# The experts' weighted sum of a two-block transformer kernel, from feature-major to token-major

## The reference, cut to what matters

```python
def peer_ffn(h, peer_wq, peer_subkeys, peer_u, peer_v):
    ...
        expert = jnp.take_along_axis(ids, pos, axis=-1)
        g = jax.nn.softmax(top_s, axis=-1).astype(hb.dtype)
        u_sel = peer_u[expert]
        a = jax.nn.gelu(jnp.einsum('bqhkd,bqd->bqhk', u_sel, hb))
        v_sel = peer_v[expert]
        return jnp.einsum('bqhk,bqhkd->bqd', g * a, v_sel)
...
        x = x + gate2 * peer_ffn(h2, peer_wq, peer_subkeys, peer_u, peer_v)
```

## Time and profile before

| | us |
|---|---|
| median of three runs (lowest, highest) | 1178.29 (1177.71, 1179.69) |
| the profiled execution: own time | 1180.36 |
| its span, first to last instruction | 1178.4 |
| PE busy in the span | 1051.1 (89%) |
| VectorE, ScalarE, GpSimd busy | 837.5, 433.0, 268.8 |
| TensorE's mean granted clock, of full speed | 0.972 |

### The profile page before, as it was taken

The page is one execution under the profiler, slowest core; times in us unless marked ns, Lnnn a source line. Parts: engine busy times, 40 slices in busy tenths (PEclk is TensorE's granted clock), DMA queues, the critical chain, the costliest instruction groups (busy, mean ns, idle before and its releaser), DMA issues.

```text
span 1178.4 us, 18884 instructions
## 1 busy us (share of the span) xinstructions
PE 1051.1 (89%) x7587; PEld 980.2 (83%) x7587; DVE 837.5 (71%) x1801; ACT 433.0 (37%) x913; POOL 268.8 (23%) x289
## 2 busy tenths in 40 slices
PE   8999987999999987777877778878999999999997
PEld 6999986998899877777877777778899888898886
DVE  7978889667667667666776766655756868765776
ACT  3635832123212221222122122211557654476452
POOL 1000005343334333333333333434000000300000
PEclk9999999999999999998999999989999999999999
DMA  9965988999999999999999999999854655455540
GB/s 371 406 244 180 348 313 307 420 421 420 421 420 420 421 420 421 420 421 420 420 420 421 420 421 422 420 422 420 325 208 161 237 205 184 147 211 179 186 171 36
DMA packets 59480, 390.35 MB, mean 331 GB/s; under 512 B 6785, under 2 KB 7809, under 8 KB 15618
## 3 DMA queue, kind: packets, MB, share of 16 engines
q0 software_dynamic: 36864, 268.45, 55.0%
q1 hardware_dynamic: 21056, 120.10, 27.8%
q10 hardware_dynamic: 1474, 0.60, 0.2%
HBM read 388.08 MB, written 1.05 MB: 330 GB/s over the span
## 4 chain that ended last, share of the span: by engine, by line
PE 63%; DMA 24%; DVE 6%; ACT 4%; issue 1%; SPq 0%; another core or an unknown queue 0%; DVEq 0%; ACTq 0%
DMA rows<-in_peer_uv,work 23%; PE aux L1566 23%; PE pj L1609 6%; PE pj L1611 5%; PE pj L1610 5%; PE aux L1545 5%; PE pj L1286 5%; PE pj L1287 4%; PE pj L1288 4%; DVE rows L2061 2%; DMA rows<-in_w_ada 1%; PE aux L1360 1%; ACT work L1142 1%; ACT rows L1010 1%; PE aux L1425 1%
## 5 line engine op out<-in xcount | busy, mean ns | idle before, releaser
L1566 PE MATMUL aux<-work,rows 128*128 128x128 f32 x2080 | 263.4, 291 | 73.8 <-ACT work L1142 73.8
L1566 PEld LDWEIGHTS aux<-work,rows 128*128 128x128 f32 x2080 | 256.2, 206 | 81.6 <-ACT work L1142 81.4
L1566 PE MATMUL aux<-work,low_pairs 128*128 128x128 f32 x2016 | 238.2, 279 | 30.2 <-ACT work L1142 30.1
L1566 PEld LDWEIGHTS aux<-work,low_pairs 128*128 128x128 f32 x2016 | 233.0, 195 | 34.0 <-ACT work L1142 34.0
L898 POOL DMA_INDIRECT rows<-in_peer_uv,work x130 | 125.5, 965 | 301.2 <-PE aux L1566 232.1
L707 DVE TENSOR_TENSOR wlo<-wring,whi 128x1024 fp32r<-128x1024 f32 x100 | 121.0, 1235 | 77.6 <-ACT whi L701 77.1
L898 POOL DMA_INDIRECT low_pairs<-in_peer_uv,work x126 | 118.3, 939 | 158.5 <-PE aux L1566 153.4
L1286 PE MATMUL pj<-xh,whi 128*128 128x256 f32 x512 | 146.3, 286 | 0.4
L1137 ACT ACTIVATE work<-work 128x4 f32<-128x4 f32 (+2 forms) x71 | 14.7, 207 | 358.3 <-DVE work L2061 358.3
L1287 PE MATMUL pj<-xl,whi 128*128 128x256 f32 x512 | 144.8, 283 | 0.0
L1288 PE MATMUL pj<-xh,wlo 128*128 128x256 f32 x512 | 144.8, 283 | 0.0
(11 more groups left out here) (288 smaller groups left out, 1461.5 us busy)
## 6 DMA issues: line engine op xcount, KB each, us to landing
wring<-in_w SPq DMA_DIRECT2D x76, 1024.0 KB, 4.8
rows<-in_w_ada SPq DMA_DIRECT2D x40, 512.0 KB, 10.1
low_pairs<-in_w_ada SPq DMA_DIRECT2D x1, 4096.0 KB, 13.4
rows<-in_w SPq DMA_DIRECT2D x3, 1024.0 KB, 10.4
rows<-in_peer_uv,work POOLq DMA_INDIRECT x130
work<-in_late_rows SPq DMA_DIRECT2D x2, 1024.0 KB, 7.5
xT<-in_gate_rows SPq DMA_DIRECT2D x2, 1024.0 KB, 7.2
rows<-in_norm_rows SPq DMA_DIRECT2D x2, 1024.0 KB, 7.3
```

The costliest lines, as they stand in the source:

```text
L1566: ins = mm(peer_sum[t][:, c * P:(c + 1) * P], pair(n)[:, D + c * P:D + (c + 1) * P], diag[:, n % PICKS, :], start=(n % (EXPERT_HEADS * PIC ...
```

## The change

The diagonal becomes the weights and v the stream: two products of 512 columns for a pair, so the sum has tokens as rows. At a tile's end it is turned back: ScalarE copies the first 512 columns of the sum from PSUM into `hT` (free by then), VectorE the other 512, TensorE turns each half with four transposes into two banks of PSUM, and `join` reads those. For tile 0 the copies come at the end of group 8, the transposes ahead of group 10's sums and the join behind group 10 (before: behind group 9). For tile 1 the first half is turned right behind the last sum, the second between the parts 3 and 4 of vg. ScalarE's copy waits for the first of the last pair's two products alone.

```diff
 def sum_pair(t, n):
     pe.wait_ge(diag_ready, n + 1)
-    for c in range(KC):
-        ins = mm(peer_sum[t][:, c * P:(c + 1) * P], pair(n)[:, D + c * P:D + (c + 1) * P], diag[:, n % PICKS, :],
-                 start=(n % (EXPERT_HEADS * PICKS) == 0 and c % 4 == 0), stop=False, skip_group_check=True)
+    of_tile = n % (EXPERT_HEADS * PICKS)
+    last = of_tile == EXPERT_HEADS * PICKS - 1
+    for c in range(2):
+        ins = mm(peer_sum[t][:, half(c)], diag[:, n % PICKS, :], pair(n)[:, D + c * 512:D + (c + 1) * 512],
+                 start=(of_tile == 0), stop=last, skip_group_check=True)
+        if last and c == 0:
+            ins.then_inc(sum_first_half, 1)
     ins.then_inc(pair_used, 1)
+
+def turn_sum(t, c):
+    pe.wait_ge(sum_out[c], t + 1)
+    for q in range(4):
+        ins = nc.tensor.transpose(aux[:, 2 + c, q * P:(q + 1) * P], hT[:, 4 * c + q, tile_of(t)], ident[:, :])
+    ins.then_inc(sum_turned, 1)
...
+                if g == EXPERT_HEADS + 2:
+                    turn_sum(0, 0)
+                    turn_sum(0, 1)
...
             pe.wait_ge(const_ready, 13)
+            pe.wait_ge(x_ready, KC)
+            turn_sum(1, 0)
...
-                    rows_pass(l, use("vg", 0), *x_tile(l, 0), at_=(2, 3))
+                    rows_pass(l, use("vg", 0), *x_tile(l, 0), at_=(2, ))
+                    turn_sum(1, 1)
+                    rows_pass(l, use("vg", 0), *x_tile(l, 0), at_=(3, ))
...
+def sum_first_half_out(t):
+    act.wait_ge(sum_first_half, t + 1)
+    nc.scalar.copy(quarter(hT, t, 0), by_chunk(peer_sum[t][:, 0:512])).then_inc(sum_out[0], 1)
...
+def sum_second_half_out(t):
+    dve.wait_ge(pair_used, (t + 1) * EXPERT_HEADS * PICKS)
+    v.tensor_copy(quarter(hT, t, 1), by_chunk(peer_sum[t][:, 512:D])).then_inc(sum_out[1], 1)
 def join(t):
     for c in range(KC):
+        if c % 4 == 0:
+            dve.wait_ge(sum_turned, 2 * t + c // 4 + 1)
         x = xT[:, c, t * P:(t + 1) * P]
-        v.scalar_tensor_tensor(x, peer_sum[t][:, c * P:(c + 1) * P], mod[:, 5 * KC + c:5 * KC + c + 1], x, ALU.mult, ALU.add) \
+        v.scalar_tensor_tensor(x, aux[:, 2 + c // 4, c % 4 * P:(c % 4 + 1) * P], mod[:, 5 * KC + c:5 * KC + c + 1], x, ALU.mult, ALU.add) \
             .then_inc(x_ready, 1)
```

More of the change, by code:

```diff
@@ L535, in build @@
         pair_used = sem("pair_used")
+        sum_first_half, sum_out, sum_turned = sem("sum_first_half"), [sem("sum_out_act"), sem("sum_out_dve")], sem("sum_turned")
         x_ready = sem("x_ready")
@@ L1157, in _ @@
                     gate_exps(g + AHEAD)
+                if g == EXPERT_HEADS:
+                    sum_first_half_out(0)
             layer_hi(act, 0, 2, 3)
+            sum_first_half_out(1)
             x0_hi(1)
@@ L2115, in _ @@
                         x0_low(0)
-                if g == EXPERT_HEADS + 1:
-                    dve.wait_ge(pair_used, EXPERT_HEADS * PICKS)
+                if g == EXPERT_HEADS:
+                    sum_second_half_out(0)
+                if g == EXPERT_HEADS + 2:
                     join(0)
             layer_lo(dve, 0, 2, 3)
-            dve.wait_ge(pair_used, LAST_PICK + 1)
+            sum_second_half_out(1)
             join(1)
```

## The result

The changed kernel took 1180.95 us, the median of 20 runs (1179.81 to 1182.78), the kernel before 1179.05 us in 20 runs beside it (1177.56 to 1182.07). The ratio is 1.0015, with a 95% interval from 1.0009 to 1.0020: slower by 1.8 us, between 1.1 and 2.4. A second measurement further down gave 1.0005 (0.9994 to 1.0015). The forecast was 1179.6 us, with a range from 1177.0 to 1182.2.

A forecast was written before the change was run, and what follows sets the result against it. The DMA gather of expert rows was taken to bound the kernel until about 820 us, then PE's chain. +2.3 us (ending) less 0.96 (earlier last sum) gave +1.3 on the median 1178.29: 1179.6 us, range 1177.0 to 1182.2.

The forecast's parts named there:

- The gather as cover: From about 200 to 820 us PE waits for expert rows, so PE time saved there is worth nothing.
- The sums: A pair's weighted sum on PE falls from 1.85 to 1.73 us, 0.12 us less a pair.
- Rivals C: 512 columns cost what four products of 128 do, so the 0.96 gain falls away: +2.3, 1180.6 us; chance 0.09.
- D: A product's time hardly grows with columns; a sum takes 0.74 us, in all -1.7, 1176.6 us; chance 0.03.
- The chain before the last sum: From 808 us, eight pairs bring 0.6 us and three later sums 0.36, so the last sum ends 0.96 us earlier.
- The limit does not bind: Last pair's landing at about 836.9 allows its diagonal at 838.65; PE reaches that sum only near 841.
- Tile 1's ending: From last sum to PE's next product, transposes and half a join take 5.2 us instead of 2.9: +2.3 us.
- 8 others, 16 records, are 1.9 us: Basis for the transposes' price in tile 1's ending: four transposes of a half take PE 0.95 us.
- The sum: Carried to the end: +2.3 for the ending less 0.96 for the earlier last sum, +1.3 us.
- Rival A: One more half-clock stretch between 836 and 849 us costs 1.7 us: +3.0, 1181.3 us; chance 0.17.
- Rival B: Fewer PE instruction blocks on the DMA engines end the gather 6.2 us earlier: 1173.4 us; chance 0.09.

The follow-up runs named there:

- second measurement: The changed kernel, unaltered, measured once more against the kernel before: ratio 1.0005 (0.9994 to 1.0015).
- new ending alone: Sums in eight products as in the kernel before, with the change's copies and transposes at the tile ends: 1180.35 us, ratio 1.0009 to the kernel before.
- half-sum kernels: Changed kernel and kernel before, each with half of a pair's products left out for most pairs: ratios 1.0028 and 1.0012 to the kernel before.
- warmed ones: Extra unused products behind each four sums of groups 11 to 14, in both kernels: before 0.9992, again 0.9991; changed 1.0004, with both halves turned at once 1.0005.

## Why the prediction was right, and where it was not

The direction and the range held: +1.3 us forecast, +1.8 (1.1 to 2.4) and +0.6 (-0.7 to +1.8) measured, and +1.0 by the tails at full clock. But that the sum came out right is in part luck: two of its terms were too large, with opposite signs.

*The gather as cover: right.* Halving PE's work there did not move the last dot. The forecast of 25 to 30 us more idle PE was too large: it is 12 us in the first pair of profiles and 10 to 11 in the later ones (111.7 and 111.8 us of waits against 100.9 and 101.6). A sum became cheaper by less than I said, by 0.07 us, which gives 17 over 248 pairs. Where the rest went is open; the granted clock from 200 to 820 us, 0.94 to 0.95 in place of 0.95 to 0.96, could have taken some of it.

*The sums: new price right, old one too high.* I took 1.73 us for the new form; it is 1.72. For the old one I took 7.41/4 = 1.85 from an early head; behind other products in the tail it is 3.57/2 = 1.79 and 1.78 to 1.80. The 7.41 has the start of a run of four in it: at full clock four old sums behind a wait take 7.42, four new ones 7.15, each 0.27 to 0.28 more than twice the 3.57 and 3.44 of two without a wait. So a pair saves 0.07, not 0.12, and part of the 0.12 was a start that both forms have. Rivals C (no saving) and D (0.74 us) fall with this. The Trainium skill (FP8 and Floating Point Precision, "TensorE Precision Notes") states that true FP32 takes four passes through the array; worked out from that, an estimate that takes one column a cycle, 1024 columns x 4 at 2.4 GHz are 1.71 us, and the measured 1.72 agrees. By that estimate the new form has almost nothing left to save, and the old one had 0.08.

*The chain before the last sum: the step that failed.* I let 0.96 us arrive, 0.6 from the eight pairs and 0.36 from the last three sums, and wrote "The limit does not bind". In the profile pair, both with a half-clock stretch, the last sum ended 843.76 - 842.68 = 1.08 us earlier, of which 805.91 - 805.54 = 0.37 is the earlier dot of pair 243, so 0.71. At full clock it is 0.2: in the five profiles with eight products a pair and no stretch the last sum ends 36.20 to 36.26 us behind the dot of pair 243, in the five with two products 36.00 to 36.04 (the kernels with half the sums left out of the count). That is the three sums at 0.07. Of the 0.6 nothing arrives. With the new ending alone the chain still holds the eight pairs, 128 records, and the small steps behind them:

```profile
806.67 14.57 PE aux L1577 x128
...
825.98 1.22 DVE wlo L708
```

In the changed kernel, measured again, a landing stands in the place of the eight pairs:

```profile
806.68 20.18 DMA low_pairs<-in_peer_uv,work
...
826.88 1.22 DVE low_pairs L2088
...
828.52 1.22 DVE wlo L708
```

Both reach VectorE's rest equally late behind the dot of pair 243, 825.98 - 804.46 = 21.52 us and 828.52 - 806.99 = 21.53: as soon as the sums get cheaper, the landing binds there.

And in front of the old ending not even the 0.2 is worth anything: 39.30 against 39.26 to 39.31. I had checked the last landing against the diagonal and PE alone. What is late next is VectorE: landing, dot, diagonal, ScalarE's rounding, VectorE's two rests, join, 844.55 - 836.25 = 8.30 us from the last dot to the vg product, with no sum in it. I had read one profile, and it happened to have the stretch, which hides this chain behind PE's.

*Tile 1's ending: right in kind, mis-sized.* Forecast 5.2 us behind the last sum in place of 2.9; it is 4.27 (4.28 without a stretch). The term is the transposes. "8 others, 16 records, are 1.9 us" was wrong: the code of that line issues 16 transposes, one record each, so four take 0.5 us and not 0.95. The rest of the chain came as forecast, the copies hidden, half a join of 1.12 us and a PE wait of 0.51 (0.4 forecast). The cost is 4.27 - 2.93 = +1.34 us with a stretch, counted from the sum's end, and 4.28 - 3.06 = +1.22 without.

*The sum.* With a stretch in both it is +1.34 - 0.71 = +0.6, and the tails say 41.41 - 40.78 = +0.6. With none it is +1.22 - 0.19 = +1.0, and the tails say 40.29 - 39.27 = +1.0. In a kernel of 1179 us the latter is a ratio of 1.0008. It lies inside the second measurement and just below the interval of the first. What the first had beyond it, 0.1 to 1.4 us, stays open: a stretch more often in the changed kernel could do it, since one costs 41.41 - 40.29 = 1.1 us there, but three profiles of each do not tell.

*Rival A* asked for a stretch between 836 and 849 us. The clock from 823 to 850 is 1.00 in both. The mechanism is real all the same, one place earlier: a stretch behind 806 us comes with 40.78 - 39.27 = 1.5 us more in the kernel before. The half-sum kernels show that stretches come with idle PE (granted clock 0.70 and 0.74 from 700 to 800 us), and the warmed ones that extra products hold them off there (1.00). That they hold them off behind 806 us is not shown by four profiles without one, since two of three have none without extra products. *Rival B* falls: q8's packets went from 33 to 10 and to 6, and the dots' first and last starts stayed 638 to 639 us apart.

## What to carry to other kernels

Work that a DMA-bound stage covered was worth nothing when it was saved, and could cost: with half of PE's work in the gather left out, its clock was lower when the backlog behind the gather began. Ahead of "the limit does not bind", follow the last landing through every engine's list up to the product that needs it, other work queued on the way (here VectorE's rests) included. When single executions scatter by more than the effect, measure from an event that both kernels share, here a late landing, to the next point that both share: the tails of the second and third profiles agreed to 0.05 us within a kernel where the spans differed by 2.3.

## What the runs showed of the hardware that was not expected

- The same program has the half-clock stretch in some executions and not in others: 0.51 of full speed from 809.0 to 812.5 us in the first profile of the kernel before, and 1.00 in the same places of the two later ones.
- Taking away about half of PE's work in the gather, its busy time from 700 to 800 us down from 79.73 to 56.47, made the changed kernel slower, 1.0028 of the kernel before against 1.0005 for the whole change, at a granted clock of 0.74 in place of 0.91.
- Four f32 transposes of 128x128 take 0.45 to 0.54 us behind products on the chain (0.65 behind a wait), and a f32 product of 512 columns 0.86, half of a pair's 1.72.
- A transfer issued 0.27 us earlier into the busy gather landed no earlier, counted from the dot of pair 243: its time from issue to landing went from 21.03 to 21.35 us.
